# A projection's last four chunks by seven half-sized products each, in a hybrid decoder step on one Trainium2 core

## What is computed

```python
h = rmsnorm(x, attn_norm_w)
xin, bg, cg, q, k, v, g_conv, g_attn = split(h @ w_in)          # w_in: 1024 x 6400
y_conv = bg * causal_conv3(cg * xin)
y_attn = window_attention(rmsnorm(q), rmsnorm(k), v)             # window 128, 16 heads, 2 kv heads, bias, sinks
x = x + (sigmoid(g_conv) * y_conv + sigmoid(g_attn) * y_attn) @ w_out
x = x + moe(rmsnorm(x))                                          # 32 experts, top 4, 1024 -> 2048 -> 1024
```

## Time and profile before

| | |
|---|---|
| median of three runs | 1162.02 us |
| the profiled execution, own time | 1162.59 us |
| its span | 1160.8 us |
| TensorE busy | 1104.7 us, 95% |
| VectorE, ScalarE, GpSimd busy | 36%, 15%, 8% |
| DMA, mean over the span | 383 GB/s |
| mean granted TensorE clock | 0.993 |

### The profile page before, as it was taken

How to read it: one execution, slowest core, us unless ns; L and a number is a source line. 1 busy time by engine, 2 the same in 40 slices (tenths; PEclk the granted TensorE clock), 3 DMA queues, 4 the chain that set the end, 5 groups by cost and what they waited for, 6 DMA issues and landing times.

```text
span 1160.8 us, 13899 instructions
## 1 busy us (share of the span) xinstructions
PE 1104.7 (95%) x5530; PEld 492.3 (42%) x5559; DVE 414.3 (36%) x851; ACT 175.0 (15%) x359; POOL 94.0 (8%) x170
## 2 busy tenths in 40 slices
PE   9999999999999999999999999999999999999997
PEld 6688888563333333333333333333333333333332
DVE  4874543463262332322323232323232323232322
ACT  2122221220131110110101010101010101010101
POOL 1755137000000000000000000000000000000000
PEclk9999999999999999999999999999999999999999
DMA  9975455769999999999999999999999999999996
GB/s 318 348 265 160 160 164 196 273 263 408 427 418 424 420 432 432 429 432 432 431 431 431 434 430 431 431 432 431 432 434 431 430 432 430 430 432 432 426 423 280
DMA packets 46110, 444.01 MB, mean 383 GB/s; under 512 B 6380, under 2 KB 12396, under 8 KB 29164
## 3 DMA queue, kind: packets, MB, share of 16 engines
q1 hardware_dynamic: 39336, 435.01, 89.8%
q0 software_dynamic: 5888, 7.88, 2.4%
q10 hardware_dynamic: 852, 0.64, 0.2%
HBM read 439.51 MB, written 2.37 MB: 381 GB/s over the span
## 4 chain that ended last, share of the span: by engine, by line
PE 59%; DMA 37%; DVE 2%; ACT 1%; issue 1%; SPq 0%; ACTq 0%
PE pB L1669 26%; PE pA L1669 26%; DMA ring<-in_w_up 16%; DMA ring<-in_w_down 12%; DMA area<-in_w_up 8%; PE pM L1669 6%; PE pM L1672 1%; DMA ring<-in_w_in 1%; PE pA L1672 1%; ACT area L1008 0%; DVE x L1521 0%; DVE hn L1563 0%; DVE area L1565 0%; DVE area L1557 0%; DVE area L1087 0%
## 5 line engine op out<-in xcount | busy, mean ns | idle before, releaser
L1669 PE MATMUL pA<-ring,hn 128*64 128x512 f32 x1536 | 352.6, 602 | 23.6 <-DMA ring<-in_w_up 23.6
L1669 PEld LDWEIGHTS pA<-ring,hn 128*64 128x64 f32 x1536 | 105.4, 137 | 219.4 <-issue 185.4
L1669 PE MATMUL pB<-area,ring 128*128 128x264 f32 (+1 forms) x928 | 182.9, 388 | 0.4 <-DMA ring<-in_w_in 0.4
L1669 PE MATMUL pB<-ring,area 128*64 128x512 f32 (+2 forms) x784 | 171.5, 591 | 7.2 <-DMA ring<-in_w_down 5.8
L1669 PEld LDWEIGHTS pB<-area,ring 128*128 128x128 f32 (+1 forms) x928 | 144.4, 175 | 35.7 <-issue 4.4
L1669 PE MATMUL pA<-area,hn 128*64 128x512 f32 x512 | 119.3, 610 | 10.4 <-DMA area<-in_w_up 10.4
L1669 PEld LDWEIGHTS pB<-ring,area 128*64 128x64 f32 (+2 forms) x784 | 58.6, 136 | 101.9 <-issue 89.0
L1521 DVE TENSOR_TENSOR x<-pM,x 128x512 f32<-128x512 f32 x60 | 40.1, 691 | 147.3 <-PE pM L1669 147.3
L996 ACT ACTIVATE area<-area 128x512 f32<-128x512 f32 x30 | 18.9, 630 | 385.4 <-DVE area L1504 385.4
L1436 DVE COPY conv_row<-pM 128x512 f32<-128x512 f32 x30 | 20.6, 686 | 146.7 <-PE pM L1669 146.7
L1669 PEld LDWEIGHTS pA<-area,hn 128*64 128x64 f32 x512 | 36.1, 139 | 74.6 <-issue 59.7
(11 more groups left out here) (306 smaller groups left out, 837.9 us busy)
## 6 DMA issues: line engine op xcount, KB each, us to landing
ring<-in_w_up SPq DMA_DIRECT2D x36, 4096.0 KB, 29.8
ring<-in_w_down SPq DMA_DIRECT2D x18, 4096.0 KB, 29.2
area<-in_w_up SPq DMA_DIRECT2D x12, 4096.0 KB, 30.2
ring<-in_w_up SPq DMA_DIRECT2D x17, 2048.0 KB, 12.6
area<-in_w_down SPq DMA_DIRECT2D x6, 4096.0 KB, 30.0
ring<-in_w_in SPq DMA_DIRECT2D x22, 1024.0 KB, 13.0
ring<-in_w_up SPq DMA_DIRECT2D x14, 1024.0 KB, 8.3
ring<-in_w_down SPq DMA_DIRECT2D x13, 1024.0 KB, 25.9
```

The costliest lines, as they stand in the source:

```text
L1669: return pe.matmul(out, w, m, start=start, stop=stop, skip_group_check=True)
```

## The change

- Chunks 9 to 12 are no longer computed by tiles. The chunk's weights are split into four blocks: input features 0-511 and 512-1023 (a11, a21 for the first 256 output features, a12, a22 for the other 256), the inputs into four blocks of 512 features x 132 tokens (b11 to b22). The four output quarters (c11 to c22) come from seven products of such blocks and sums of them, the Winograd form of Strassen's scheme: four sums of weights and four of inputs before, and sums of products behind.
- A product ("slot" s of chunk c) is 8 matmuls of 132 columns. Banks: X and Y are the two of `pB`, U and V lie in `pA`.
- The weight sums s1 to s4 (each 128 x 1024 elements) are made by GpSimd, one instruction each, for one chunk after another, and take a ring slot per chunk; `RING` gives the new order of slots. The sums of inputs are made by VectorE after tiles 24 and 33 ("sides"), into the place of `qT`, a part of `hn` and, for the last, in place in `hT`.
- ScalarE copies product 0 to SBUF; VectorE adds the products up; sigmoids and gating work on quarters (2 x 132 columns).
- The steps that stood after tiles 34 to 49 stand after certain slots.
- The blocks of units 1 to 3 and the 24 copies of bias parts are halved between the queues of GpSimd and SyncE. The order of the first expert pieces is changed.

```diff
-FIRST_ORDER = [0, 10, 1, 2, 11, 3, 7, 4, 5, 6, 8, 9]
+FIRST_ORDER = [0, 1, 11, 2, 3, 10, 7, 4, 5, 6, 8, 9]
+MOVED_BEFORE = {10: 1, 12: 2, 13: 3}
...
-def place(c):
-    return (c + 3) % SLOTS
+SEVEN = (9, 10, 11, 12)
+RING = [(what, c) for c in range(FIRST_CHUNKS) for what in (("w", "s") if c in SEVEN else ("w",))]
+def place(c, what="w"):
+    return (RING.index((what, c)) - len(RING)) % SLOTS
...
+def before(c, what="w"):
+    r = RING.index((what, c)) - SLOTS
+    return RING[r][1] + 1 if r >= 0 else 0
...
 UNIT_STEPS = [(11, 12, 12, 13, 13, 18, 19), (18, 18, 19, 20, 21, 27, 28),
-              (26, 27, 28, 29, 30, 36, 37), (35, 36, 37, 37, 38, 42, 43)]
+              (26, 27, 28, 29, 30, slot(9, 4), slot(10, 2)),
+              (slot(9, 0), slot(9, 1), slot(9, 2), slot(9, 2), slot(10, 1), slot(10, 6), slot(11, 1))]
+SPLIT_STEPS = [slot(10, 3), slot(10, 4), slot(10, 5)]
+CONV_STEP = slot(9, 5)
...
+def moves_of(u, queue):
+    return (moves(u)[::2], moves(u)[1::2])[queue] if u else (moves(u), [])[queue]
...
-        steps.append(("tile", n))
-        steps += after[n]
+        if TILES[n][1] not in SEVEN:
+            steps.append(("tile", n))
+            steps += after[n]
+    for c in SEVEN:
+        for s in range(7):
+            steps.append(("slot", (c, s)))
+            steps += after[slot(c, s)]
...
+        t1, r1, w_, c_, s_ = (b.rearrange("p (a n) -> p a n", a=2) for b in (tmp[:, 0, :], tmp[:, 1, :], rt[:], kT, vT))
+        bank_x, bank_y = pB[:, 0, 0:NT], pB[:, 1, 0:NT]
+        bank_u, bank_v = pA[:, 1024:1024 + NT], pA[:, 1536:1536 + NT]
+        b11, b12 = hT[:, 0:K2, 0:HALF], hT[:, 0:K2, HALF:NT]
+        b21, b22 = hT[:, K2:KT, 0:HALF], hT[:, K2:KT, HALF:NT]
+        side1 = qT[:, 0:2, :].rearrange("p k n -> p (k n)").rearrange("p (k n) -> p k n", k=K2)
+        side2 = qT[:, 2:4, :].rearrange("p k n -> p (k n)").rearrange("p (k n) -> p k n", k=K2)
+        side4 = hn[:, 1, 256:256 + K2 * HALF].rearrange("p (k n) -> p k n", k=K2)
+        side3 = b12
...
+            def move_blocks(u):
+                sp.wait_ge(staging_cleared, 2)
+                sp.wait_ge(prob_ready, u + 1)
+                sp.wait_ge(probT_ready, u)
+                for b, qi, kj in moves_of(u, 1):
+                    dst = stage[b][32 * kj:32 * kj + 32].rearrange("p (h a c) -> p h a c", h=8, a=4)[:, :, qi]
+                    src = prob[32 * qi:32 * qi + 32, :, 128 * b + 32 * kj:128 * b + 32 * kj + 32]
+                    sp.dma_start(dst, src).then_inc(moved_by_sync, 16)
             for c in range(2, FIRST_CHUNKS):
-                if c >= SLOTS:
-                    sp.wait_ge(ring_free, c - SLOTS + 1)
+                if c in MOVED_BEFORE:
+                    move_blocks(MOVED_BEFORE[c])
+                if before(c):
+                    sp.wait_ge(ring_free, before(c))
...
+            sp.wait_ge(misc_free, FILL["values", 3])
+            sp.wait_ge(bias_cast, SPLITS)
+            for c in range(3):
+                for q in (2, 3):
+                    part = slice(32 * q, 32 * q + 32)
+                    sp.dma_start(bias_up[32 * c:32 * c + 32, 512 * q:512 * q + 512], up_parts[part, c]).then_inc(moved_by_sync, 16)
+                    sp.dma_start(bias_down[32 * c:32 * c + 32, 256 * q:256 * q + 256], down_parts[c][part]).then_inc(moved_by_sync, 16)
...
                 if j == 10:
+                    sp.wait_ge(sig_used, 2 * KT)
                     sp.wait_ge(misc_free, FILL["values", 3])
                     sp.wait_ge(blocks_turned, CONV_TURNED)
...
+            def add_weights(i, c):
+                a11, a12, a21, a22 = weights(c)
+                s1, s2, s3, s4 = weight_sums(c)
+                pool.wait_ge(ring_full[place(c)], filled(c))
+                pool.wait_ge(ring_free, before(c, "s"))
+                def combine(out, a, b, op):
+                    nc.gpsimd.tensor_tensor(out, a, b, op).then_inc(sums_ready, 1)
+                combine(s1, a21, a22, ALU.add)
+                combine(s3, a11, a21, ALU.subtract)
+                pool.wait_ge(sums_ready, 4 * i + 1)
+                combine(s2, s1, a11, ALU.subtract)
+                pool.wait_ge(sums_ready, 4 * i + 3)
+                combine(s4, a12, s2, ALU.subtract)
...
-                for b, qi, kj in moves(u):
+                for b, qi, kj in moves_of(u, 0):
...
+            add_weights(0, SEVEN[0])
+            add_weights(1, SEVEN[1])
             move_blocks(2)
-            move_blocks(3)
+            add_weights(2, SEVEN[2])
             pool.wait_ge(blocks_turned, CONV_TURNED)
             for q in range(4):
...
+            move_blocks(3)
+            add_weights(3, SEVEN[3])
...
             for c in range(3):
...
-                for q in range(4):
+                for q in range(2):
...
+                elif what == "slot":
+                    c, s = a
+                    gated = (c, "c22") in ACT_DONE
+                    if s == 0:
+                        act.wait_ge(tile_full, FULL[c, 0])
...
+                        nc.scalar.activation(t1, pairs_of(bank_x), ACT.Copy).then_inc(tile_free_act, 1)
+                    elif s == 2 and gated:
...
+                        act.wait_ge(tile_free_dve, DVE_READ[c, "r1"])
...
+                        nc.scalar.activation(s_, pairs_of(bank_x), ACT.Sigmoid).then_inc(tile_free_act, 1)
+                    elif s >= 4 and gated:
+                        name, b = (("c22", c_), ("c12", w_), ("c21", r1))[s - 4]
+                        act.wait_ge(tile_free_dve, DVE_READ[c, name])
+                        nc.scalar.activation(b, b, ACT.Sigmoid).then_inc(tile_free_act, 1)
...
+            def finish(c, name):
+                nonlocal freed
+                kind = TILES[2 + 4 * (c - 1)][0]
+                g = {"c11": s_, "c22": c_, "c12": w_, "c21": r1}[name]
+                out = quarter(yc, c, name)
+                dve.wait_ge(tile_free_act, ACT_DONE[c, name])
+                if kind == "gc":
+                    dve.wait_ge(tile_free_dve, DVE_READ[c, "r1"])
+                    V.tensor_tensor(out, g, out, ALU.mult).then_inc(sig_used, 1)
+                else:
+                    dve.wait_ge(sig_used, freed)
+                    dve.wait_ge(misc_free, misc.n)
+                    link(V.tensor_tensor(g, g, quarter(ya, c, name), ALU.mult))
+                    V.tensor_tensor(out, g, out, ALU.add).then_inc(sig_used, 1)
+                freed += 1
+                assert freed == GATED[c, name]
+            def seven(c, s):
+                gated = (c, "c22") in ACT_DONE
+                def read(name, out, a, b):
+                    V.tensor_tensor(out, a, pairs_of(b), ALU.add).then_inc(tile_free_dve, 1)
+                def times(name, g):
+                    dve.wait_ge(tile_free_dve, DVE_READ[c, name])
+                    out = quarter(yc, c, name)
+                    link(V.tensor_tensor(out, g, out, ALU.mult))
+                if s == 0:
+                    if (c - 1, "c21") in GATED:
+                        finish(c - 1, "c21")
+                    return
+                if s != 2 or not gated:
+                    dve.wait_ge(tile_full, FULL[c, s])
+                if s == 1:
+                    dve.wait_ge(tile_free_act, ACT_DONE[c, "t1"])
+                    if (c - 1, "c21") in GATED:
+                        dve.wait_ge(sig_used, GATED[c - 1, "c21"])
+                    read("r1", r1, t1, bank_y)
+                elif s == 2 and not gated:
+                    out = quarter(yc, c, "c11")
+                    V.tensor_tensor(out, pairs_of(bank_x), out, ALU.mult).then_inc(tile_free_dve, 1)
+                elif s == 3:
+                    read("w", w_, t1, bank_y)
+                elif s == 4:
+                    dve.wait_ge(tile_free_dve, DVE_READ[c, "w"])
+                    read("c22", c_, w_, bank_u)
+                    if not gated:
+                        times("c22", c_)
+                elif s == 5:
+                    read("c12", w_, w_, bank_v)
+                    if gated:
+                        finish(c, "c22")
+                    else:
+                        times("c12", w_)
+                elif s == 6:
+                    if gated:
+                        finish(c, "c12")
+                    read("c21", r1, r1, bank_u)
+                    if not gated:
+                        times("c21", r1)
+                    else:
+                        finish(c, "c11")
+                        if c == LAST:
+                            finish(c, "c21")
             freed = 0
             for what, a in STEPS:
-                if what == "anorm":
+                if what == "slot":
+                    seven(*a)
+                elif what == "sides":
+                    if a == 0:
+                        V.tensor_tensor(side1, b12, b11, ALU.subtract).then_inc(h_ready, 1)
+                        dve.wait_ge(h_ready, KT + 1)
+                        V.tensor_tensor(side2, b22, side1, ALU.subtract).then_inc(h_ready, 1)
```

(51 more changed lines are left out.)

95 lines of the change are left out of this document (80 added, 15 removed).

## The result

The changed kernel takes 1176.79 us (median of four runs, 1175.77 to 1179.34) beside 1162.75 for the kernel before on the same chip: a ratio of 1.0126, 95% interval [1.0114, 1.0138], 14.0 us slower. The forecast was 1156.0. The execution that was profiled is the slowest of the four, 1179.34 us.

What follows compares the result with a forecast made beforehand. TensorE bounds the changed stage, and time saved before 222 us moves the expert-weight stream one for one. Products save 6.0 us, the stage's end 0.5, waits take 0.5: 6.0 off, median 1156.0, range 1153.8 to 1162.0.

Steps and rivals of the forecast that it cites:

- Cost nothing, covered by 10 us or more: GpSimd's sixteen weight sums for chunks 9 to 12, 2.4 us each, are ready before their products and add no time.
- Rival (a): VectorE's two-SBUF-input instructions and GpSimd's sums block each other: 3.4 us lost, 2.6 saved, 1159.4; chance 0.25.
- The sign of being wrong: In chunk 9 onward, TensorE idle before product 3 or 6, put down to VectorE, would point to blocking or late reads.
- The products at 1.82 us: Chunks 9 to 12: each product 16 x 0.111 + 0.04 us; 28 products take 51.0 against 57.0, saving 6.0.
- Chunk 9 to the output in 55 us: Sign of being right: chunk 9 to the output in about 55 us, first output product near 203.
- The 2.9 us of slack before product 3: Chunk 9: VectorE can be 1.8 + 1.15 us late before product 3 is delayed.
- The second queue is needed: Unit 2's blocks need SyncE too, issued in 5.8 instead of 11.6 us, since unit 3's bias overwrites them at 153.0.
- the 0.5 us taken off for waits: Allowance in chunks 9 to 12 for VectorE waits that the working could not place: 0.5 us less gain.
- (b): GpSimd's sums too slow, delaying unit 2's blocks: gain gone at 4.1 us per sum, 1165.5 at 4.5; chance 0.11.
- (e): VectorE's reads come late throughout, 0.2 us at each of 28 products: 5.6 lost, 1161.6; chance 0.07.
- slow products: Chunks 9 to 12: short matmuls take 0.135 us each, products total 61.6 against 57.0: 4.1 slower, 1166; chance 0.05.
- stream that takes back more of the gain: Seven expert-weight pieces at 300 GB/s end at 239, so the stream starts as late as before: 1162; chance 0.05.

Runs made afterwards that it cites:

- the placed kernel: Changed kernel with waits so GpSimd's sums start after all input differences, unit 3's maximum and chunk 10's last gating: 1155.91 us, ratio 0.994.
- this clash alone: The placed kernel with its third-set wait removed, so those sums start right behind the moves of unit 2: 1164.76 us, ratio 1.0017.
- the kernel without sums: Changed kernel with GpSimd's weight sums left out, products reading blocks of the chunk itself instead: 1156.06 us, ratio 0.994.
- one clash at a time: Three kernels, each the placed kernel with one wait removed, for the first eight sums, third set or fourth set: 1160.81, 1164.76, 1166.94 us.
- the kernel with short sums: Changed kernel with each sum issued as four instructions of 256 columns: 1165.28 us, ratio 1.0049.
- the changed kernel with pauses: Changed kernel where each GpSimd sum also waits until the sum before it is finished: 1169.24 us, ratio 1.0049.
- three waits: Changed kernel whose GpSimd sums wait for three input differences, the fourth difference (third set) and the second bias split (last set): 1164.77 us, ratio 1.0017.

## Why the prediction was wrong

**The step that failed** is the one on GpSimd's sums, "Cost nothing, covered by 10 us or more". Their length (2.47 us for 2.4), their number and their deadlines were right; that they cost VectorE nothing was wrong. In the places where the change put them they cost 20.9 us, the difference between the changed kernel and the placed one. The step asked only when GpSimd has time and when TensorE needs the sums, never which VectorE instructions run meanwhile.

**Rival (a)** named the mechanism, with a chance of 0.25 and a price of 3.4 us. It was short on four counts:
- Places. It weighed the third set beside the tap steps and the fourth beside chunk 10. It missed the first eight sums beside the input differences after tile 24 (4.9 us), because the working for them looked at GpSimd's idle 24 us alone; and beside the fourth set it saw the gatings, not the two subtractions that split the expert biases.
- The count of holds. It took two at the third set; there were four in the changed kernel, for which its own scale gives 6.7 us. Measured were 5.09, and 5.65 with this clash alone. At the fourth set it gave 1.5; measured were 6.9 to 7.1. It also took all six tap steps for steps with two SBUF inputs; two have one (TENSOR_SCALAR) and are held all the same.
- The length of a hold. It took one sum. An instruction can be held for three, 7.0 us or more.
- The clock. After each of the three gaps TensorE works at the lower level for a while. Against the undisturbed rows the records behind the three gaps are longer by 1.5, 2.0 and 2.8 us, 6.3 of the 21.6 us at the output start; the gaps are 15.0. No term of the sum had this.

**The sign of being wrong** that the prediction named, idle time before product 3 or 6 put down to VectorE, is there twice (5.09 before product 3 of chunk 9, 6.90 before product 6 of chunk 10). The third gap, before the values of unit 1, lies ahead of chunk 9, where it did not look.

**What held.** The products at 1.82 us: 1.80. Chunk 9 to the output in 55 us and the output near 203: 202.63 and 202.51 without holds. The 2.9 us of slack before product 3: 3.2. 6.0 us off: 6.5. That the placed kernel ends within 0.1 us of 1156.0 is partly luck: at the output start it is 7.2 us ahead of the kernel before, since 28 products saved 0.6 us more than forecast and the 0.5 us taken off for waits was not needed, and some 0.7 us of that are lost again behind it. The second queue is needed: yes, though for the turn of unit 3 rather than the bias step. Rivals (b) to (e) are out: sums of 2.5 us, no slow products, no stream that takes back more of the gain than that 0.7 us, no late reads in the kernel without sums.

The prediction put rival (a) beside a rule of the Trainium skill (SBUF — State Buffer, "Who interferes with whom"). By that rule the trace agrees in kind: sums hold instructions with two SBUF inputs, memsets do not; the one-input tap steps are held by memsets too, which the rule gives for VectorE's two-port modes (whether these steps ran in one, the trace does not say); a read with one input in PSUM is free. By the rule the one issued first has the ports for its whole length and the other waits for it; here a waiting one also stood through the two sums issued after it.

## What to carry to other kernels

Work put on GpSimd isn't beside VectorE's just because GpSimd has time: list the VectorE instructions that run meanwhile with two SBUF inputs (or TENSOR_SCALAR steps on SBUF data), and count each as held until the GpSimd instruction beside it ends, whatever its own size: mostly 1.2 to 2.7 us here, with sums of 2.3, and 7 us or more where one was held through three. Look for a stretch without them and tie the work to its start by a semaphore; one wait in the right place was worth 5 to 11 us here. And price an idle time of TensorE above its length: with one clash at a time the output started 1.4 to 3.5 us later than the idle time alone gives, most of it work at the lower clock. The length of the gap alone does not tell: behind 3.36 us idle in the kernel with short sums the granted clock was 1.00, behind 2.28 us in the changed kernel with pauses 0.52.

## What the runs showed of the hardware that was not expected

- A VectorE instruction that meets an unbroken row of GpSimd sums may be held through three of them (7.04, 7.24, 8.16, 9.28 us; the last two records begin 0.6 and 2.1 us ahead of the first sum); with a real wait of GpSimd between the sums none was held for more than 3.6. In other rows without that wait one was let in after a single sum (2.39 in the changed kernel, 2.48 with three waits); what decides was not found.
- Write-only GpSimd instructions leave two-input VectorE instructions at their 0.71 us but hold one-input steps of SBUF data (TENSOR_SCALAR of 256 columns and of 8) for their whole 2.3 us.
- The hold does not depend on size: an instruction of 8 elements per partition lasts 2.2 us where it takes 0.17.
- GpSimd's sums last longer too where VectorE comes in between: the first eight 20.24 us in the changed kernel, 18.97 in the placed one.
- Splitting the sums to 256 columns raises their total from 39.2 to 48.5 us and the kernel's time scatters over 12 us (1161.3 to 1173.8).
